# Two more weight places for the experts, laid at the end of the work area

## The chip, the cores and the metric

The kernel runs on one core of a Trainium2 chip. The metric is the device time of one execution in microseconds (us). The program is one launch, written engine by engine: TensorE (PE), VectorE (DVE), ScalarE (ACT), GpSimd (POOL) and the sync engine (SP) each have their own instruction stream, and they meet only at semaphores.

## The reference

Three transformer blocks follow one another on 256 tokens of width 1024, all in float32. The change concerns the mixture of experts of the first block: 32 experts, four of them for each token.

```python
def clamped_swiglu(gu):
    gate = jnp.minimum(gu[..., :D_FF], SWIGLU_LIMIT)
    lin = jnp.clip(gu[..., D_FF:], -SWIGLU_LIMIT, SWIGLU_LIMIT)
    return gate * jax.nn.sigmoid(SWIGLU_ALPHA * gate) * (lin + 1)

def moe_ffn(h, w_router, b_router, w_gu, b_gu, w_down, b_down):
    logits = (h @ w_router + b_router).astype(jnp.float32)
    top_val, top_idx = lax.top_k(logits, TOP_K)
    gate_w = jax.nn.softmax(top_val, axis=-1).astype(h.dtype)
...
    def expert_block(args):
        xb, e = args
        gu = xb @ w_gu[e] + b_gu[e]
        return clamped_swiglu(gu) @ w_down[e] + b_down[e]
```

Each expert has a w_gu of 1024 x 2048 and a w_down of 1024 x 1024, 12 MiB together.

## The kernel before

**Weights.** All weights of the three blocks lie in HBM as one stream of pieces, each 128 partitions x 2048 float32, 1 MiB. A ring in SBUF has four places (`SLOTS`). SP alone loads it: it waits until `pieces_used` says that the piece that lay in a place four pieces earlier has been multiplied, then issues one DMA for the next piece into that place. TensorE waits on the semaphore of the place (`ring_full_0` to `_3`) before it multiplies, and raises `pieces_used` behind the piece's last matmul. Piece n lies in place n % 4.

**Experts.** With these inputs no expert has more than 64 tokens, apart from the fullest one, which is run twice; so the `narrow` path runs: 33 items (`ITEMS`), one after another, in a hardware loop on each engine. An item is 12 pieces, j0 to j11: j0 to j7 are w_gu (L793), j8 to j11 are w_down (L822). What TensorE does in an item, in its order:

- j0 and j1 (L793); the scatter of the item before (`scatter`, L761); its exit matrix turned (`exits`, L767)
- j2 and j3; the gather of the next item's tokens (`gather`, L751); a turned block of the hidden rows (`turned`, L772)
- j4 and j5; a turned block; j6 and j7; two turned blocks
- j8 to j11 (L822); then the next item's j0

ACT copies the hidden rows out of PSUM (L2168), makes the sigmoids (L2173) and copies the result of an item (L2189), and DVE does the bias, the clamps and the products (L1548 to L1559). The last of the 33 items repeats the fullest expert: SP reads its number with one load of a value (L1279) and issues the 12 pieces from lines of its own (L1282).

**The work area.** `work` is one tensor of 128 partitions x 32768 float32 in which each stage lays its own tiles. From the places that `plan` takes for the first block, its mixing part reaches column 27528 and the `narrow` path column 20117.

Of the kernel before, what the change touches and what calls it, by code (L numbers as in the profile page):

```python
# [30 lines left out]
D = 1024  # L31
DC = D // P
HD = 64
SLOTS = 4
SLOT = 2048
SCALE = HD ** -0.5
MASKED = -1e30
# [115 lines left out]
def build(nc, stages, dram, known):  # L153
# [6 lines left out]
    with ctx:  # L160
# [86 lines left out]
            return got  # L247


        ring_full = [sem(f"ring_full_{s}") for s in range(SLOTS)]  # L250
        used = signal("pieces_used")
        ones_set, silu_of_c = signal("ones_set"), signal("silu_of_c")
        masks_set = signal("masks_set")
# [239 lines left out]
        def _(pe):  # L493
# [7 lines left out]
            def piece(name, i=0):  # L501

                n = place[name, i]
                pe.wait_ge(ring_full[n % SLOTS], 16 * (n // SLOTS + 1))
                return ring[:, n % SLOTS, :]

            def conditioning(s, a, b, fresh=False):

# [226 lines left out]
            def narrow(m):  # L735
# [45 lines left out]
                with pe.Fori(0, ITEMS) as e:  # L781
                    for i in range(4):
                        if i == 0:
                            pe.wait_ge(nar_xe, e + 1)
                        if i >= 2:
                            pe.wait_ge(nar_g, e * 4 + (i - 1))
                        for h in range(2):
                            n = base + 2 * i + h
                            pe.wait_ge(ring_full[n % SLOTS], e * 48 + 16 * (n // SLOTS + 1))
                            w = ring[:, n % SLOTS, :].rearrange("p (c g o) -> p c g o", c=4, g=2)  # L790
                            for c in range(4):
                                for g in range(2):
                                    mm = pe.matmul(psum[g * SEATS:(g + 1) * SEATS, 4 + i % 2, 0:256],  # L793
                                                   m["xe"][:, 4 * h + c, :], w[:, c, g, :],
                                                   start=(h == 0 and c == 0), stop=True, skip_group_check=True)
                            mm.then_inc(used.sem, 1)
                        if i == 0:
                            pe.wait_ge(nar_y, e + 1)
                            scatter()
                            pe.wait_ge(nar_ge, e + 1)  # L800
                            exits()
                        if i == 1:
                            pe.wait_ge(nar_lv, e + 1)
                            pe.wait_ge(nar_en, e + 2)
                            gather()
                        if i >= 1:
                            pe.wait_ge(nar_g, e * 4 + i)
                            if i >= 2:
                                pe.wait_ge(nar_b, e * 4 + (i - 1))
                            turned(i - 1)  # L810
                    pe.wait_ge(nar_g, e * 4 + 4)
                    pe.wait_ge(nar_b, e * 4 + 3)
                    turned(3)
                    pe.wait_ge(nar_xe, e + 2)
                    for k in range(4):
                        n = base + 8 + k
                        pe.wait_ge(ring_full[n % SLOTS], e * 48 + 16 * (n // SLOTS + 1))
                        pe.wait_ge(nar_act, e * 4 + (k + 1))
                        w = ring[:, n % SLOTS, :].rearrange("p (f o) -> p f o", f=2)
                        for f in range(2):  # L820
                            for h in range(2):
                                mm = pe.matmul(psum[h * SEATS:(h + 1) * SEATS, 7, :], m["act_e"][:, 2 * k + f, :],  # L822
                                               w[:, f, h * 512:(h + 1) * 512], start=(k == 0 and f == 0), stop=True,
                                               skip_group_check=True)
                        mm.then_inc(used.sem, 1)
# [3 lines left out]
            def wide(m):  # L829
# [13 lines left out]
                with pe.Fori(0, E_N) as e:  # L843
                    for j in range(8):
                        n = base + j
                        pe.wait_ge(ring_full[n % SLOTS], e * 48 + 16 * (n // SLOTS + 1))
                        h = j % 2
                        if h == 0:
                            pe.wait_ge(moe_free, e * 8 + (j + 2))
                        w = ring[:, n % SLOTS, :].rearrange("p (c g o) -> p c g o", c=4, g=2)  # L850
                        for k in range(2):
                            for g in range(2):
                                for c in range(4):
                                    mm = pe.matmul(psum[:, 4 + (j - h + k) % 4, g * T:(g + 1) * T],
                                                   w[:, c, g, k * P:(k + 1) * P], hT[:, 4 * h + c, :],
                                                   start=(h == 0 and g == 0 and c == 0), stop=True,
                                                   skip_group_check=True)
                        mm.then_inc(used.sem, 1)
                    for k in range(4):
                        n = base + 8 + k  # L860
                        pe.wait_ge(ring_full[n % SLOTS], e * 48 + 16 * (n // SLOTS + 1))
                        pe.wait_ge(moe_v, e * 40 + 5 * (2 * k + 2))
                        w = ring[:, n % SLOTS, :].rearrange("p (f o) -> p f o", f=2)
                        for f in range(2):
                            for c in range(DC):
                                mm = pe.matmul(acc[:, c, :], w[:, f, c * P:(c + 1) * P], m["act"][:, 2 * k + f, :],
                                               start=False, stop=False, skip_group_check=True)
                        mm.then_inc(used.sem, 1)
                for k in range(12):

                    n = base + 12 * E_N + k
                    pe.wait_ge(ring_full[n % SLOTS], 16 * (n // SLOTS + 1))
# [379 lines left out]
        def _(sp):  # L1252
            stream = dram["stream"]

            def send(n, k):

                sp.wait_ge(used.sem, n - SLOTS + 1)
                sp.dma_start(ring[:, n % SLOTS, :], stream[k]).then_inc(ring_full[n % SLOTS], 16)

            def sent(first, last, back):  # L1260

# [7 lines left out]
                for n in range(b * SLOTS, last):  # L1269
                    send(n, n - back)  # L1270

            for s in range(SLOTS):
                sp.dma_start(ring[:, s, :], stream[s]).then_inc(ring_full[s], 16)
            if 1 in stages:
                base = first_piece["moe"]
                again = base + 12 * E_N
                sent(SLOTS, again, 0)
                sp.wait_ge(*at("flag_set"))
                fullest = sp.value_load(A[1]["flag"][0:1, 1:2], min_val=0, max_val=E_N - 1)  # L1279
                for k in range(12):  # L1280
                    sp.wait_ge(used.sem, again + k - SLOTS + 1)
                    sp.dma_start(ring[:, (again + k) % SLOTS, :], stream[fullest * 12 + (base + k)]) \  # L1282
                      .then_inc(ring_full[(again + k) % SLOTS], 16)
                sent(again + 12, n_pieces, 12)
            else:
                sent(SLOTS, n_pieces, 0)

# [3 lines left out]
        def _(ve):  # L1291
# [521 lines left out]
            def peer():  # L1813
# [92 lines left out]

                def u_low(s):

                    slot = (first_piece["peer"] + s) % SLOTS
                    ve.tensor_tensor(ring_parts[:, slot, 0:D], ring[:, slot, 0:D], m["u_high"][:, s % 2, :].bitcast(F32), ALU.subtract) \  # L1910
                      .then_inc(blk_ul, 1)

                ve.wait_ge(*at("zeroed"))
# [11 lines left out]
                def block(s, n, last=False):  # L1925

                    if not last:
# [12 lines left out]
                    slot = (first_piece["peer"] + s) % SLOTS  # L1940
                    ve.wait_ge(blk_h, n + 1)
                    ve.tensor_tensor(ring_parts[:, slot, D:2 * D], ring[:, slot, D:2 * D], m["v_high"][:, s % 2, :].bitcast(F32), ALU.subtract) \  # L1942
                      .then_inc(blk_w, 1)

                with ve.Fori(0, PE_N // 4 - 1) as i:
# [101 lines left out]
        def _(sc):  # L2047
# [235 lines left out]
            def peer():  # L2283
# [51 lines left out]
                def landed(s):  # L2335
                    return ring_full[(base + s) % SLOTS], 16 * ((base + s) // SLOTS + 1)

                sc.wait_ge(*landed(0))
                u_high(0)
                for s in range(4):  # L2340

                    sc.wait_ge(*landed(s + 1))
                    if s >= 1:
                        sc.wait_ge(blk_a, s)
                    u_high(s + 1)
# [3 lines left out]
                    gelu(s)  # L2349
                with sc.Fori(1, PE_N // 4 - 1) as i:  # L2350
                    for s in range(4):
                        full, count = landed(s + 1)
# [6 lines left out]
                for s in range(4):  # L2359
                    n = PE_N - 4 + s  # L2360
                    if s < 3:
                        sc.wait_ge(*landed(n + 1))
# [339 lines left out]
```

## Time and profile before

| | us |
|---|---|
| median of 3 runs | 3379.26 |
| lowest and highest run | 3374.78, 3379.7 |
| profiled execution, its own time | 3371.07 |
| its span in the trace | 3369.3 |

The page of the profile gives, for 40 equal slices of the span (84.2 us each), how busy each engine was, the TensorE clock that was granted, and what the DMA engines moved. Counted from 0, slices 6 to 16 lie wholly in the experts' stage. A view of windows gives the same numbers for any stretch, the timeline gives the instructions in order, each with the idle time before it and what ended that, and the view of one tile tells how long a DMA took from its issue to its landing. Ends of matmuls are modelled, so starts are the firmer reading.

### The profile page before, as it was taken

To read this page: it belongs to the slowest core of one execution; us is meant where nothing else is said; L and a number is where in the kernel's file an instruction comes from. 1 tells how busy PE (TensorE), PEld (TensorE's weight loads), DVE (VectorE), ACT (ScalarE), POOL (GpSimd) and SP (SyncE) were. 2 spreads that over 40 slices of the span, in tenths; PEclk is the share of its full clock that TensorE was granted. 3 is DMA by queue.
4 is the path that set the end of the run, shared out by engine and by line. 5 is a ranking of instruction groups with operands and counts; after the bars stand their busy time and mean duration, and the time that the engine had idled before them with its cause. 6 is when DMAs were issued, how large, how long until landed. Compare 5 with 4: busy or idle time off the path is not lost.

```text
span 3369.3 us, 55104 instructions
## 1 busy us (share of the span) xinstructions
PE 3013.5 (89%) x21350; PEld 2375.7 (71%) x21350; DVE 1281.4 (38%) x2809; ACT 867.9 (26%) x1464; POOL 127.3 (4%) x85
## 2 busy tenths in 40 slices
PE   7999899999999999988999518899999999889998
PEld 5678655555455454547788417799999999767887
DVE  1520212122221222222411589866666666521330
ACT  2310112212222222221411004444444444321110
POOL 0000000000000000000000016500000000000000
PEclk9999889999999999999999759999999999879999
DMA  5664579999999999984654200045545555423342
GB/s 233 263 252 155 197 297 386 398 385 392 397 386 397 389 384 398 377 360 152 236 221 142 88 0 0 0 167 182 187 176 185 183 178 186 164 75 125 138 150 88
DMA packets 105299, 763.89 MB, mean 227 GB/s; under 512 B 11776, under 2 KB 11776, under 8 KB 12672
## 3 DMA queue, kind: packets, MB, share of 16 engines
q1 hardware_dynamic: 103536, 753.97, 58.3%
q0 software_dynamic: 1680, 8.72, 0.7%
q8 instruction: 63, 1.03, 0.1%
q14 instruction: 20, 0.16, 0.0%
HBM read 760.55 MB, written 2.10 MB: 226 GB/s over the span
## 4 chain that ended last, share of the span: by engine, by line
PE 79%; DMA 9%; DVE 8%; issue 2%; ACT 1%; DVEq 0%; POOL 0%; SPq 0%; ACTq 0%; POOLq 0%
PE psum L554 20%; PE psum L793 13%; PE psum L1163 11%; PE psum L1172 11%; DMA weight_ring<-in_stream 9%; PE psum L751 4%; PE psum L822 3%; DVE chunkbuf L1887 3%; PE psum L1229 2%; PE psum L570 2%; PE psum L761 2%; PE psum L516 2%; PE psum L545 1%; PE psum L772 1%; DVE work L1293 1%
## 5 line engine op out<-in xcount | busy, mean ns | idle before, releaser
L793 PE MATMUL psum<-weight_ring,work 128*64 128x256 f32 x4224 | 494.5, 384 | 37.0 <-DMA weight_ring<-in_stream 36.2
L554 PE MATMUL psum<-hT,weight_ring 128*128 128x256 f32 x2240 | 505.0, 388 | 15.5 <-ACT hT L2049 15.5
L554 PEld LDWEIGHTS psum<-hT,weight_ring 128*128 128x128 f32 x2240 | 436.0, 195 | 80.9 <-issue 18.7
L793 PEld LDWEIGHTS psum<-weight_ring,work 128*64 128x64 f32 x4224 | 290.0, 137 | 226.5 <-DMA weight_ring<-in_stream 78.9
L1548 DVE TENSOR_TENSOR work<-psum,work 128x256 f32<-128x256 f32 x132 | 56.2, 426 | 810.6 <-PE psum L772 810.6
L822 PE MATMUL psum<-weight_ring,work 128*64 128x512 f32 x1056 | 248.2, 602 | 28.7 <-DMA weight_ring<-in_stream 28.4
L1172 PE MATMUL psum<-peer_parts,v_high 128*128 128x256 f32 x2048 | 266.8, 283 | 0.3 <-DVE ring_parts L1942 0.2
L1172 PEld LDWEIGHTS psum<-peer_parts,v_high 128*128 128x128 f32 x2048 | 254.9, 192 | 0.7 <-DVE ring_parts L1942 0.7
L822 PEld LDWEIGHTS psum<-weight_ring,work 128*64 128x64 f32 x1056 | 66.6, 136 | 186.8 <-DMA weight_ring<-in_stream 96.8
L554 PE MATMUL psum<-work,weight_ring 128*128 128x256 f32 x800 | 175.9, 382 | 5.4 <-DVE work L1293 3.0
L1922 DVE TENSOR_TENSOR chunkbuf<-chunkbuf,work 128x256 f32<-128x256 f32 x128 | 81.7, 638 | 240.0 <-ACT chunkbuf L2324 240.0
L554 PEld LDWEIGHTS psum<-work,weight_ring 128*128 128x128 f32 x800 | 152.9, 192 | 27.6 <-DVE work L1293 3.8
L2049 ACT ACTIVATE work<-psum 128x512 f32<-128x512 f32 (+4 forms) x107 | 67.5, 638 | 381.8 <-PE psum L554 338.0
L1910 DVE TENSOR_TENSOR ring_parts<-weight_ring,peer_parts 128x1024 fp32r<-128x1024 f32 x128 | 156.8, 1225 | 15.3 <-ACT peer_parts L2332 10.7
L2332 ACT ACTIVATE peer_parts<-weight_ring 128x1024 fp32r<-128x1024 f32 x128 | 135.9, 1063 | 94.6 <-DMA weight_ring<-in_stream 94.6
L1942 DVE TENSOR_TENSOR ring_parts<-weight_ring,v_high 128x1024 fp32r<-128x1024 f32 x128 | 156.0, 1219 | 0.0
L1887 DVE TENSOR_TENSOR chunkbuf<-vec,chunkbuf 128x512 f32<-128x512 f32 x128 | 153.7, 1246 | 4.9 <-PE psum L1120 3.3
L1163 PE MATMUL psum<-h_high,peer_parts 128*128 128x256 f32 x1024 | 144.9, 284 | 4.9 <-DVE ring_parts L1910 4.9
L2168 ACT ACTIVATE work<-psum 128x256 f32<-128x256 f32 x132 | 51.1, 387 | 368.9 <-PE psum L793 368.9
L1163 PE MATMUL psum<-h_low,peer_parts 128*128 128x256 f32 x1024 | 144.5, 284 | 0.0
L1163 PE MATMUL psum<-h_high,ring_parts 128*128 128x256 f32 x1024 | 144.5, 284 | 0.0
L1172 PE MATMUL psum<-peer_parts,ring_parts 128*128 128x256 f32 x1024 | 143.7, 283 | 0.0
(251 smaller groups left out, 3626.1 us busy)
## 6 DMA issues: line engine op xcount, KB each, us to landing
weight_ring<-in_stream SPq DMA_DIRECT2D x719, 1024.0 KB, 6.5
work<-in_rows POOLq DMA_DIRECT2D x1, 1312.0 KB, 16.9
xT<-in_x POOLq DMA_DIRECT2D x1, 1024.0 KB, 9.8
work<-in_ctx POOLq DMA_DIRECT2D x1, 1024.0 KB, 18.9
x_spill<-xT POOLq DMA_DIRECT2D x1, 1024.0 KB, 7.4
xT<-x_spill POOLq DMA_DIRECT2D x4, 256.0 KB, 6.8
out_x<-xT POOLq DMA_DIRECT2D x4, 256.0 KB, 2.9
work<-in_moe POOLq DMA_DIRECT2D x1, 768.0 KB, 6.7
```

Source lines behind the costliest of these rows:

```text
L554: mm = pe.matmul(ps[:, j * T:(j + 1) * T], w[:, c, j * P:(j + 1) * P], moving[:, c, :], start=(j == 0 and c == 0), stop=True, skip_group_c ...
L751: mm = pe.matmul(psum[:, 7, c * SEATS:(c + 1) * SEATS], m["x_nat"][:, t, c * P:(c + 1) * P], m["en"][:, t, :], start=(c == 0 and t == 0), ...
L793: mm = pe.matmul(psum[g * SEATS:(g + 1) * SEATS, 4 + i % 2, 0:256], m["xe"][:, 4 * h + c, :], w[:, c, g, :], start=(h == 0 and c == 0), st ...
L822: mm = pe.matmul(psum[h * SEATS:(h + 1) * SEATS, 7, :], m["act_e"][:, 2 * k + f, :], w[:, f, h * 512:(h + 1) * 512], start=(k == 0 and f = ...
L1163: mm = pe.matmul(psum[:, 4 + s % 4, 0:T], u[:, c * P:(c + 1) * P], h[:, c, :], start=(k == 0 and c == 0), stop=True, skip_group_check=True)
L1172: mm = pe.matmul(acc[:, c, :], v[:, c * P:(c + 1) * P], m[wt][:, s % 2, :], start=False, stop=False, skip_group_check=True)
L1887: ve.tensor_tensor(place, m["v"]["iota"].unsqueeze(1).to_broadcast([P, CHUNK, PE_N]), m["idxT"][:, q, bass.ds(at0 + t * P, CHUNK)].unsquee ...
L1910: ve.tensor_tensor(ring_parts[:, slot, 0:D], ring[:, slot, 0:D], m["u_high"][:, s % 2, :].bitcast(F32), ALU.subtract) \
L1922: ve.tensor_tensor(m["wt"][:, s % 2, :], m["ge"][:, s % 2, :], G[:, :, bass.ds(n, 1)].rearrange("p t a -> p (t a)"), ALU.mult).then_inc(bl ...
L1942: ve.tensor_tensor(ring_parts[:, slot, D:2 * D], ring[:, slot, D:2 * D], m["v_high"][:, s % 2, :].bitcast(F32), ALU.subtract) \
L2049: sc.activation(out_, in_, func, **kw).then_inc(*A_.up(*names))
L2332: sc.activation(m["u_high"][:, s % 2, :], ring[:, (base + s) % SLOTS, 0:D], ACT.Copy) \
```

## The change

While the experts run, the ring has six places instead of four (`MORE = 2`). Places 4 and 5 are the last 4096 columns of `work`, from column 28672. Within an item, piece j lies in place j % 6 (for places below four, counted from where the ring stands), and 12 is a multiple of six, so that every item finds its pieces in the same places. SP issues a piece of the experts when the piece six before it has been multiplied. For the first item j0 to j3 go out under the old condition, j4 and j5 directly behind j3, and from j6 on the new condition holds. Behind the experts the ring has four places again. `landed` works out what the semaphore of a place counts to, and `landed_of` does it for item e of a loop.

```diff
 SLOTS = 4
+MORE = 2
 SLOT = 2048
...
-        ring_full = [sem(f"ring_full_{s}") for s in range(SLOTS)]
+        ring_full = [sem(f"ring_full_{s}") for s in range(SLOTS + MORE)]
+
+
+        moe_at = first_piece["moe"]
+        moe_end = moe_at + 12 * ITEMS
+        more = work[:, 32768 - MORE * SLOT:32768].rearrange("p (s k) -> p s k", s=MORE)
+        assert moe_at % SLOTS == moe_end % SLOTS and 12 % (SLOTS + MORE) == 0
+        loads = 12 // (SLOTS + MORE)
+
+        def place_of(n):
+            if moe_at <= n < moe_end:
+                s = (n - moe_at) % 12 % (SLOTS + MORE)
+                return s if s >= SLOTS else (moe_at + s) % SLOTS
+            return n % SLOTS
+
+        def slot(n):
+            s = place_of(n)
+            return ring[:, s, :] if s < SLOTS else more[:, s - SLOTS, :]
+
+        def landed(n):
+
+            s = place_of(n)
+            if n < moe_at:
+                return ring_full[s], 16 * (n // SLOTS + 1)
+            past = len([k for k in range(moe_at) if k % SLOTS == s]) if s < SLOTS else 0
+            if n < moe_end:
+                e, j = divmod(n - moe_at, 12)
+                return ring_full[s], 16 * (past + loads * e + j // (SLOTS + MORE) + 1)
+            return ring_full[s], 16 * (past + loads * ITEMS + (n - moe_end) // SLOTS + 1)
+
+        def landed_of(n, e):
+
+            full, count = landed(n)
+            return full, e * (16 * loads) + count
...
                n = place[name, i]
-                pe.wait_ge(ring_full[n % SLOTS], 16 * (n // SLOTS + 1))
-                return ring[:, n % SLOTS, :]
+                pe.wait_ge(*landed(n))
+                return slot(n)
...
                            n = base + 2 * i + h
-                            pe.wait_ge(ring_full[n % SLOTS], e * 48 + 16 * (n // SLOTS + 1))
-                            w = ring[:, n % SLOTS, :].rearrange("p (c g o) -> p c g o", c=4, g=2)
+                            pe.wait_ge(*landed_of(n, e))
+                            w = slot(n).rearrange("p (c g o) -> p c g o", c=4, g=2)
...
                        n = base + 8 + k
-                        pe.wait_ge(ring_full[n % SLOTS], e * 48 + 16 * (n // SLOTS + 1))
+                        pe.wait_ge(*landed_of(n, e))
                         pe.wait_ge(nar_act, e * 4 + (k + 1))
-                        w = ring[:, n % SLOTS, :].rearrange("p (f o) -> p f o", f=2)
+                        w = slot(n).rearrange("p (f o) -> p f o", f=2)
...
                 sp.wait_ge(used.sem, n - SLOTS + 1)
-                sp.dma_start(ring[:, n % SLOTS, :], stream[k]).then_inc(ring_full[n % SLOTS], 16)
+                sp.dma_start(slot(n), stream[k]).then_inc(landed(n)[0], 16)
...
+            def item(at_once, piece_of, e=0):
+
+                for j in range(12):
+                    n = moe_at + j
+                    if at_once and j >= SLOTS + MORE:
+                        sp.wait_ge(used.sem, n - (SLOTS + MORE) + 1)
+                    elif at_once and j < SLOTS:
+                        sp.wait_ge(used.sem, n - SLOTS + 1)
+                    elif not at_once:
+                        sp.wait_ge(used.sem, e * 12 + (n - (SLOTS + MORE) + 1))
+                    sp.dma_start(slot(n), piece_of(j)).then_inc(landed(n)[0], 16)
+
             for s in range(SLOTS):
                 sp.dma_start(ring[:, s, :], stream[s]).then_inc(ring_full[s], 16)
             if 1 in stages:
-                base = first_piece["moe"]
-                again = base + 12 * E_N
-                sent(SLOTS, again, 0)
+                sent(SLOTS, moe_at, 0)
+                item(True, lambda j: stream[moe_at + j])
+                with sp.Fori(1, E_N) as e:
+                    item(False, lambda j: stream[e * 12 + (moe_at + j)], e)
                 sp.wait_ge(*at("flag_set"))
                 fullest = sp.value_load(A[1]["flag"][0:1, 1:2], min_val=0, max_val=E_N - 1)
-                for k in range(12):
-                    sp.wait_ge(used.sem, again + k - SLOTS + 1)
-                    sp.dma_start(ring[:, (again + k) % SLOTS, :], stream[fullest * 12 + (base + k)]) \
-                      .then_inc(ring_full[(again + k) % SLOTS], 16)
-                sent(again + 12, n_pieces, 12)
+                item(False, lambda j: stream[fullest * 12 + (moe_at + j)], E_N)
+                sent(moe_end, n_pieces, 12)
```

The same two replacements are made in `wide`, which does not run here, and two names that the new functions would hide are changed on DVE and ACT.

The instructions of SP, from the end of the pieces ahead of the experts, before. The loop of L1268 sends every piece up to the last but one item, four at a time; L1282 sends the repeated expert.

```order
L1268 ISA [waits pieces_used]
L1268 DMA weight_ring<-in_stream 128x2048
L1265 REGISTER_ALU
L1265 COMPARE_AND_BRANCH
L1279 TENSOR_LOAD work [waits vector_done_ffn1]
L1279 ISA x2
L1282 ISA [waits pieces_used]
L1282 DMA weight_ring<-in_stream 128x2048
```

The same place in the changed kernel: the first item's twelve pieces, and the start of the loop over the other items (L1316; the branch is L1323's).

```order
L1316 DMA weight_ring<-in_stream 128x2048 [waits pieces_used] x4
L1316 DMA work<-in_stream 128x2048 x2
L1316 DMA weight_ring<-in_stream 128x2048 [waits pieces_used] x4
L1316 DMA work<-in_stream 128x2048 [waits pieces_used] x2
L1323 UNCONDITIONAL_BRANCH
L1323 ISA
L1316 ISA [waits pieces_used]
L1316 DMA weight_ring<-in_stream 128x2048
```

SP's code is longer, and the two DMAs into `work` of the first item wait for nothing of their own. The number and the order of the pieces are the same.

TensorE at the end of an item (j8 to j11), before:

```order
L822 MATMUL psum<-weight_ring,work 64x512 [waits narrow_activations,ring_full_0]
L822 MATMUL psum<-weight_ring,work 64x512 x3
L822 MATMUL psum<-weight_ring,work 64x512 [waits narrow_activations,ring_full_1]
L822 MATMUL psum<-weight_ring,work 64x512 x3
L822 MATMUL psum<-weight_ring,work 64x512 [waits narrow_activations,ring_full_2]
L822 MATMUL psum<-weight_ring,work 64x512 x3
L822 MATMUL psum<-weight_ring,work 64x512 [waits narrow_activations,ring_full_3]
L822 MATMUL psum<-weight_ring,work 64x512 x3
```

and in the changed kernel:

```order
L856 MATMUL psum<-weight_ring,work 64x512 [waits narrow_activations,ring_full_2,narrow_tokens_copied]
L856 MATMUL psum<-weight_ring,work 64x512 x3
L856 MATMUL psum<-weight_ring,work 64x512 [waits narrow_activations,ring_full_3]
L856 MATMUL psum<-weight_ring,work 64x512 x3
L851 REGISTER_ALU
L856 MATMUL psum<-work 64x512 [waits narrow_activations,ring_full_4]
L856 MATMUL psum<-work 64x512 x3
L856 MATMUL psum<-work 64x512 [waits narrow_activations,ring_full_5]
L856 MATMUL psum<-work 64x512 x3
```

The matmuls stand as before. The last two pieces are read from `work`, and their semaphores are those of the new places.

## Rows read from the trace of the kernel before

**Rows 1.** The page, busy tenths in 40 slices, and rates

```profile
PE   7999899999999999988999518899999999889998
...
PEclk9999889999999999999999759999999999879999
DMA  5664579999999999984654200045545555423342
GB/s 233 263 252 155 197 297 386 398 385 392 397 386 397 389 384 398 377 360 152 236 221 142 88 0 0 0 167 182 187 176 185 183 178 186 164 75 125 138 150 88
```

**Rows 2.** Windows: the experts, two stretches of one item, a later stage

```profile
core 0: us, PE busy (x) PEld busy (x) DVE busy (x) ACT busy (x) POOL busy (x), PEclk, DMA share, GB/s
434.50:1500.20 1065.70, 977.07 (x7194) 555.60 (x7194) 230.98 (x792) 225.16 (x428) 0.00 (x0) 1.00 0.96 387
717.00:742.00 25.00, 22.83 (x162) 12.75 (x164) 3.39 (x13) 5.24 (x9) 0.00 (x0) 1.00 1.01 424
742.00:748.00 6.00, 6.00 (x56) 3.70 (x52) 3.03 (x11) 0.73 (x3) 0.00 (x0) 1.00 0.79 264
...
2200.00:2900.00 700.00, 700.00 (x5835) 700.00 (x5835) 452.09 (x610) 291.76 (x365) 0.00 (x0) 1.00 0.51 182
```

**Rows 3.** Waits from 434.5 to 1500.3: total us, times, longest

```profile
PEld psum L822 <- DMA weight_ring<-in_stream: 96.8, 89, 1.7
...
PEld psum L793 <- DMA weight_ring<-in_stream: 78.9, 64, 2.1
...
PE psum L793 <- DMA weight_ring<-in_stream: 36.2, 64, 1.2
...
PE psum L822 <- DMA weight_ring<-in_stream: 28.4, 58, 0.8
```

**Rows 4.** Timeline of PE, 700 to 770: start, length, instructions, idle before

```profile
700.32 0.44 PE L767 MATMUL psum<-ident,work 128*128 128x128 f32 x2
...
708.23 3.67 PE L793 MATMUL psum<-weight_ring,work 128*64 128x256 f32 x32
711.83 0.44 PE L772 MATMUL psum<-ident,work 128*128 128x128 f32 x2
...
717.30 3.67 PE L822 MATMUL psum<-weight_ring,work 128*64 128x512 f32 x16
721.52 1.94 PE L822 MATMUL psum<-weight_ring,work 128*64 128x512 f32 x8 [0.55 <-DMA weight_ring<-in_stream]
724.00 1.94 PE L822 MATMUL psum<-weight_ring,work 128*64 128x512 f32 x8 [0.55 <-DMA weight_ring<-in_stream]
726.47 1.95 PE L793 MATMUL psum<-weight_ring,work 128*64 128x256 f32 x16 [0.53 <-DMA weight_ring<-in_stream]
728.96 1.95 PE L793 MATMUL psum<-weight_ring,work 128*64 128x256 f32 x16 [0.55 <-DMA weight_ring<-in_stream]
730.84 2.00 PE L761 MATMUL psum<-work 64*128 64x256 f32 x16
732.77 0.44 PE L767 MATMUL psum<-ident,work 128*128 128x128 f32 x2
...
749.75 3.65 PE L822 MATMUL psum<-weight_ring,work 128*64 128x512 f32 x16
...
762.90 2.00 PE L761 MATMUL psum<-work 64*128 64x256 f32 x16
764.83 0.43 PE L767 MATMUL psum<-ident,work 128*128 128x128 f32 x2
```

**Rows 5.** Issue to landing, four loads issued 723 to 732

```profile
DMA to landing us min/median/max: 7.8/7.8/7.8
```

**Rows 6.** The same, one load issued at 742.8

```profile
DMA to landing us min/median/max: 5.2/5.2/5.2
```

**Rows 7.** The same, six loads issued 403 to 416

```profile
DMA to landing us min/median/max: 7.5/9.5/10.0
```

**Rows 8.** Timeline of ACT and DVE around j8 to j0

```profile
719.37 0.29 DVE L1559 TENSOR_TENSOR work<-work 128x128 f32<-128x128 f32 x1
...
725.99 0.60 ACT L2189 ACTIVATE work<-psum 128x512 f32<-128x512 f32 x1 [6.90 <-PE psum L822]
726.61 1.28 ACT L2168 ACT_TABLE_LOAD   x1
```

**Rows 9.** Timeline of PE: first j0, last pieces, what follows

```profile
434.50 6.11 PE L793 MATMUL psum<-weight_ring,work 128*64 128x256 f32 x32 [0.77 <-ACT work L2157]
...
1498.29 1.94 PE L822 MATMUL psum<-weight_ring,work 128*64 128x512 f32 x8 [0.56 <-DMA weight_ring<-in_stream]
1500.92 2.00 PE L761 MATMUL psum<-work 64*128 64x256 f32 x16 [0.70 <-ACT work L2189]
1507.88 5.36 PE L545 MATMUL psum<-work,ones 128*128 128x256 f32 x16 [4.96 <-ACT work L2049]
```

More of the change, by code:

```diff
@@ L845, in wide @@
                         n = base + j
-                        pe.wait_ge(ring_full[n % SLOTS], e * 48 + 16 * (n // SLOTS + 1))
+                        pe.wait_ge(*landed_of(n, e))
                         h = j % 2
@@ L849, in wide @@
                             pe.wait_ge(moe_free, e * 8 + (j + 2))
-                        w = ring[:, n % SLOTS, :].rearrange("p (c g o) -> p c g o", c=4, g=2)
+                        w = slot(n).rearrange("p (c g o) -> p c g o", c=4, g=2)
                         for k in range(2):
@@ L860, in wide @@
                         n = base + 8 + k
-                        pe.wait_ge(ring_full[n % SLOTS], e * 48 + 16 * (n // SLOTS + 1))
+                        pe.wait_ge(*landed_of(n, e))
                         pe.wait_ge(moe_v, e * 40 + 5 * (2 * k + 2))
-                        w = ring[:, n % SLOTS, :].rearrange("p (f o) -> p f o", f=2)
+                        w = slot(n).rearrange("p (f o) -> p f o", f=2)
                         for f in range(2):
@@ L871, in wide @@
                     n = base + 12 * E_N + k
-                    pe.wait_ge(ring_full[n % SLOTS], 16 * (n // SLOTS + 1))
+                    pe.wait_ge(*landed(n))
                     pe.matmul(psum[0:1, 4, 0:2], ones[:, 0:1], ones[:, 0:2], start=True, stop=True,
@@ L1907, in u_low @@
                 def u_low(s):
-                    slot = (first_piece["peer"] + s) % SLOTS
-                    ve.tensor_tensor(ring_parts[:, slot, 0:D], ring[:, slot, 0:D], m["u_high"][:, s % 2, :].bitcast(F32), ALU.subtract) \
+                    at0 = (first_piece["peer"] + s) % SLOTS
+                    ve.tensor_tensor(ring_parts[:, at0, 0:D], ring[:, at0, 0:D], m["u_high"][:, s % 2, :].bitcast(F32), ALU.subtract) \
                       .then_inc(blk_ul, 1)
@@ L1938, in block @@
                     ve.tensor_tensor(low, wt, high.bitcast(F32), ALU.subtract).then_inc(blk_w, 1)
-                    slot = (first_piece["peer"] + s) % SLOTS
+                    at0 = (first_piece["peer"] + s) % SLOTS
                     ve.wait_ge(blk_h, n + 1)
-                    ve.tensor_tensor(ring_parts[:, slot, D:2 * D], ring[:, slot, D:2 * D], m["v_high"][:, s % 2, :].bitcast(F32), ALU.subtract) \
+                    ve.tensor_tensor(ring_parts[:, at0, D:2 * D], ring[:, at0, D:2 * D], m["v_high"][:, s % 2, :].bitcast(F32), ALU.subtract) \
                       .then_inc(blk_w, 1)
@@ L2333, in u_high, with in_ring @@
                       .then_inc(blk_uh, 1)
-                def landed(s):
-                    return ring_full[(base + s) % SLOTS], 16 * ((base + s) // SLOTS + 1)
-                sc.wait_ge(*landed(0))
+                def in_ring(s):
+                    return landed(base + s)
+                sc.wait_ge(*in_ring(0))
                 u_high(0)
                 for s in range(4):
-                    sc.wait_ge(*landed(s + 1))
+                    sc.wait_ge(*in_ring(s + 1))
                     if s >= 1:
@@ L2351, in peer @@
                     for s in range(4):
-                        full, count = landed(s + 1)
+                        full, count = in_ring(s + 1)
                         sc.wait_ge(full, i * 16 + count)
@@ L2361, in peer @@
                     if s < 3:
-                        sc.wait_ge(*landed(n + 1))
+                        sc.wait_ge(*in_ring(n + 1))
                         sc.wait_ge(blk_a, n)
```

## The prediction, as it was made before the changed kernel ran

> **What bounds the kernel now.** I read the page first. TensorE is busy nearly everywhere, and in the experts' slices, 6 to 16 counted from 0, the DMA engines are too (a 9 in each, 377 to 398 GB/s); in no other stage do both stand high [rows 1]. So the experts have two candidates for a bound, and an average over slices can't choose between them. The windows give the stage's measure: from the first j0 at 434.50 to the end of the last j11 at 1498.29 + 1.94 = 1500.23 [rows 9] it takes 1065.7 us, 32.29 us for each of 33 items, at 387 GB/s, and with TensorE busy for 977 us [rows 2].
>
> Then I looked inside one item. From 717 to 742 the DMA engines move 424 GB/s, from 742 to 748 only 264 [rows 2]. The reader is to see that the link isn't at its limit all the time: once in each item it runs short of requests. The waits of the stage say that TensorE in turn waits for loads: 36.2 + 28.4 us before matmuls, in 64 + 58 waits, all of them on the ring [rows 3]. The timeline shows where. After j3 and the long gather the ring is full and TensorE sets the pace; at 721.52, 724.00, 726.47 and 728.96 each piece (j10, j11, j0, j1) starts only when its load has landed [rows 4]. So in one half of an item the link starves for places, in the other TensorE starves for pieces. That is what a ring too short for uneven use looks like. The two costs are one: what the link loses at 742 is missing when j9 to j1 want it.
>
> **How fast could each of the two go alone.**
>
> TensorE: two pieces without a wait take 711.83 - 708.23 = 3.60 us. The six pieces j8 to j1 take 730.84 - 717.30 = 13.54 us where 3 x 3.60 = 10.80 would do. The whole item, from L767 to L767, took 764.83 - 732.77 = 32.06 us, and the one ahead of it 732.77 - 700.32 = 32.45. In the item of 32.06 the six pieces took 762.90 - 749.75 = 13.15 [rows 4]. Without the waits: 32.06 - 2.35 = 29.71, and 32.45 - 2.74 = 29.71 us.
>
> Link: three landings in a row are 728.96 - 721.52 = 7.44 us apart [rows 4], 2.48 us for each 1 MiB piece, or 29.76 us for twelve. By the window, 12 x 1.0486 MB / 424 GB/s = 29.68 us [rows 2].
>
> So both limits are about 29.7 us, 2.5 us under today's item.
>
> **What six places do.** From 730.84 to 749.75 TensorE works 18.91 us on six pieces and other matmuls [rows 4], and the link could bring 18.91 / 2.48 = 7.6 pieces. In the next six pieces, 10.80 us, it brings 4.35. About 1.65 pieces must be stored over the item. With four places, one is being multiplied and one lies empty for the time that a load needs from issue to landing beyond its own 2.48 us: 5.2 us in all for a load that finds nothing ahead of it [rows 6]. Two are left for the 1.65, and those two also hold the loads in flight. The link's loss of 32.29 - 29.76 = 2.53 us per item is one piece. Two more places are more than that piece, and more than the 1.65. A load then waits longer behind others, which costs nothing: with three in flight it lands after 7.8 us [rows 5], and where SP sent more, ahead of the experts, after up to 10.0 [rows 7], which is 2.2 us, less than one landing interval, more.
>
> **The sum.** As both limits nearly coincide, a landing that comes late isn't caught up by a faster partner, so I take 29.9 us per item, 0.14 over the larger of the two. The first item starts at half the clock: its first two pieces take 6.11 us and not 3.67 [rows 9, 4], 2.4 us that stay. New stage: 33 x 29.9 + 2.4 = 989.1 us. Gain: 1065.7 - 989.1 = 76.6 us.
>
> *Bounds of the unknown terms.* At best 29.71 us per item: 982.8, a gain of 82.9. At worst for a part that the trace doesn't show: TensorE never went from j11 to j0 without a wait for a load, so the loop's end may hold a cost of its own; it is at most 726.47 - 724.00 - 1.80 = 0.67 us, which would make 30.4 us and a gain of 60.1. I take nearly nothing for it, because the later stage with loops of matmuls shows 700.00 us busy in 700 [rows 2].
>
> *Costed at nothing.* (1) What other engines do for TensorE in the shortened half. The last activation for j11 is ready at 719.37 + 0.29 = 719.66; j11 would start at 717.30 + 5.40 = 722.70. The result of an item is copied (0.60 us) and a table loaded (1.28) within 1.90 us of the last piece's end [rows 8]; the scatter that reads the copy stands two pieces later, 3.60 us, and the first hidden rows are copied then, too. Cover left: 1.7 us. (2) SP's longer code, its extra register instructions and the load of the fullest expert's number: up to five requests are now ahead of TensorE, over 9 us. (3) j4 and j5 of the first item, sent early: 5 us of link time between 415 and 434.5, in which TensorE doesn't wait for the link. (4) What follows: the first piece behind the experts is sent on the same condition as before, and TensorE goes from 1500.92 through waits for ACT [rows 9] that no load takes part in; the rest moves forward as a block.
>
> The profiled execution took 3371.07 us, the median of the runs is 8.2 us over it, and I keep that distance: 3371.07 - 76.6 + 8.2 = 3302.7, forecast **3302 us**.
>
> **One rule weighed.** The windows hold 424 GB/s over 25 us and 387 over the stage [rows 2]; this is what the second limit rests on. The Trainium skill (HBM Reference, Specifications (TRN2)) gives about 425 GB/s for a core that streams alone, set by its 16 DMA engines; by that estimate twelve pieces take 29.6 us and the gain would be 1065.7 - 33 x 29.71 - 2.4 = 82.9, TensorE being the slower then.
>
> **The rivals.**
>
> *The link has less to give than a 25 us window promises.* The DMA engines' busy share is 0.96 over the stage [rows 2]; if busy means full, only 0.04 x 1065.7 = 43 us are left: 3336 us. If the 264 GB/s at 742 is the memory's own hiccup after a burst, nothing is left: 3379. Against both: the dip comes once per item, behind the gather, when SP has nothing to send, and the share reads 1.01 where 424 GB/s move and still 0.79 where 264 do, so it counts packets that are slow to start. The Trainium skill (DMA: Bandwidth & Descriptors, Where 436 GB/s comes from) says that loads from HBM are held to about 358 GB/s by the memory; by that rule the stage would be past its limit already and nothing would change. The stage's 387 GB/s says otherwise. Chances: 0.10 for the first, 0.07 for no change.
>
> *Another engine's chain takes the wait's place.* If the 1.7 us of cover is not there, or the loop's end costs more than 0.67 us, an item takes 30.4 to 31 us: 3319 to 3339 us. 0.08.
>
> *Slower: TensorE's clock.* It works with fewer pauses, and the granted clock could fall in this stage. Below 29.71 / 32.29 = 0.92 the item is longer than now; at 0.90 it is 33.0 us, the stage 1091.8, the time 3405 us. Against it: 700 us with TensorE busy throughout at a granted 1.00 [rows 2]. The lower digits stand at the stages' seams, where it pauses [rows 1]. 0.03.
>
> **How the numbers follow.** The forecast's own range, 29.7 to 30.4 us per item, is 3296 to 3319 us and has 0.70; 0.02 is for a larger gain. The range for 8 in 10 takes in most of the other engine's chain and a few us of spread between runs: 3290 to 3334. Two runs of this kernel differ by 5 us, so 0.2%, 7 us, is about what can be told from no change. Faster by more: 0.70 + 0.02 + 0.10 + 0.08 = 0.90; within: 0.07; slower: 0.03.
>
> **What would show it.** In the changed kernel's profile an item, L795 to L795, takes 29.7 to 30.2 us, and the stage ends near 1424. Over the stage the link moves 415 GB/s or more, with no stretch of 6 us below 380. The waits of TensorE for loads fall from 122 to a few tens, short ones, or it waits as often but briefly, if the link is the slower by a hair. Loads land 10 to 15 us after their issue, still 2.48 us apart. Wrong, if landings move apart, if the clock of the stage is below 1.00, or if a new wait (ACT's copy before L795, the table load) stands at the item's seam. All stages from 1500 on keep their lengths.

## The result, and the profile after

| | before | changed |
|---|---|---|
| median, us | 3377.02 (4 runs, 3374.0 to 3379.7) | 3284.74 (4 runs, 3282.43 to 3287.05) |
| profiled execution, its own time | 3371.07 | 3284.36 |
| its span | 3369.3 | 3282.6 |
| the experts, first j0 to end of last j11 | 1065.7 | 984.3 |
| the span without them | 2303.6 | 2298.3 |

The ratio is 0.9727 with a 95% interval of 0.971 to 0.9744. Forecast were 3302 us and a range of 3290 to 3334. The direction and the mechanism hold; the time lies 5.3 us under the range.

The page of the changed kernel, busy tenths and rates in 40 slices, answers to [rows 1]:

```profile
PE   7999899999999999989999058899999999789998
...
DMA  5664489999999999956634000155445555423442
GB/s 240 260 266 148 169 330 422 422 422 422 422 422 422 422 422 422 422 198 264 241 142 150 17 0 0 52 180 186 183 179 181 186 182 179 143 82 124 146 149 90
```

Eleven slices in a row, 6 to 16, read exactly 422 GB/s, where they read 377 to 398 before, and windows of 6 us, from 464 to 506 and from 1380 to 1410, read 418 to 429, so the dip once in each item is gone. (The link is the path from HBM through the DMA engines to SBUF.) The windows of the stage, and of two stretches of 25 us, answer to [rows 2]; the clock stays at 1.00, 2.4 GHz:

```profile
core 0: us, PE busy (x) PEld busy (x) DVE busy (x) ACT busy (x) POOL busy (x), PEclk, DMA share, GB/s
433.00:1417.30 984.30, 954.82 (x7194) 564.86 (x7194) 230.94 (x792) 224.77 (x428) 0.00 (x0) 1.00 1.00 417
700.00:725.00 25.00, 24.04 (x198) 15.43 (x196) 5.35 (x19) 6.52 (x12) 0.00 (x0) 1.00 1.01 422
725.00:750.00 25.00, 24.78 (x190) 14.80 (x188) 4.35 (x15) 5.33 (x9) 0.00 (x0) 1.00 1.01 422
```

The timeline of TensorE in an item of the first six, and in a later one (start, length, instructions, idle time before); it answers to [rows 4]:

```profile
529.20 0.44 PE L801 MATMUL psum<-ident,work 128*128 128x128 f32 x2
...
546.18 3.65 PE L856 MATMUL psum<-weight_ring,work 128*64 128x512 f32 x16
549.67 3.60 PE L856 MATMUL psum<-work 128*64 128x512 f32 x16
553.10 3.62 PE L827 MATMUL psum<-weight_ring,work 128*64 128x256 f32 x32
556.65 2.00 PE L795 MATMUL psum<-work 64*128 64x256 f32 x16
558.58 0.44 PE L801 MATMUL psum<-ident,work 128*128 128x128 f32 x2
```

```profile
737.27 0.44 PE L801 MATMUL psum<-ident,work 128*128 128x128 f32 x2
...
761.17 1.90 PE L827 MATMUL psum<-weight_ring,work 128*64 128x256 f32 x16
763.29 1.95 PE L827 MATMUL psum<-weight_ring,work 128*64 128x256 f32 x16 [0.22 <-DMA weight_ring<-in_stream]
765.17 2.00 PE L795 MATMUL psum<-work 64*128 64x256 f32 x16
767.10 0.44 PE L801 MATMUL psum<-ident,work 128*128 128x128 f32 x2
```

The early item takes 558.58 - 529.20 = 29.38 us without a wait. There the six pieces j8 to j1, 546.18 to 556.65, take 10.47 us (13.15 and 13.54 before). The later one takes 767.10 - 737.27 = 29.83, with a short wait at j0 and at j1. Twelve landings at 2.485 us are 29.82. So the stage has two parts: up to the sixth item TensorE sets the pace, from the seventh on the link. The waits of TensorE for loads from 610 to 1417.3 answer to [rows 3] (total us, times, longest); of the 64.6 us before matmuls (PE), 5.8 are left, and of the 175.7 before weight loads (PEld), 27.1:

```profile
PEld psum L827 <- DMA weight_ring<-in_stream: 27.1, 54, 0.7
PE psum L827 <- DMA weight_ring<-in_stream: 5.8, 27, 0.2
```

A load into the four places of the ring now takes this long from issue to landing, 610 to 1400, where a queued one took 7.8 us before [rows 5]; one into the two new places takes 8.4 to 11.7:

```profile
DMA to landing us min/median/max: 9.3/11.0/12.8
```

### The profile page after: what moved, and what is told of

The parts are those of the page before. It is cut to its first block, busy times and chain, and to the rows that moved or that the text cites. A ratio compares the mean times of both kernels' runs of the same rounds, so it can differ in the third digit from the quotient of the medians.

```text
span 3282.6 us, 54818 instructions
## 1 busy us (share of the span) xinstructions
PE 2987.1 (91%) x21350; PEld 2382.4 (73%) x21350; DVE 1281.0 (39%) x2809; ACT 866.6 (26%) x1464; POOL 127.3 (4%) x85
## 4 chain that ended last, share of the span: by engine, by line
PE 78%; DMA 10%; DVE 8%; issue 2%; ACT 1%; DVEq 0%; POOL 0%; SPq 0%; ACTq 0%; POOLq 0%
PE psum L588 21%; PE psum L827 13%; PE psum L1197 11%; PE psum L1206 11%; DMA weight_ring<-in_stream 9%; PE psum L785 4%; DVE chunkbuf L1931 3%; PE psum L1263 2%; PE psum L604 2%; PE psum L795 2%; PE psum L550 2%; PE psum L579 2%; PE psum L856 1%; DVE work L1337 1%; ACT work L2093 1%
## 5 line engine op out<-in xcount | busy, mean ns | idle before, releaser
L827 PE MATMUL psum<-weight_ring,work 128*64 128x256 f32 x3168 | 370.7, 384 | 6.6 <-DMA weight_ring<-in_stream 5.8
L827 PEld LDWEIGHTS psum<-weight_ring,work 128*64 128x64 f32 x3168 | 220.3, 137 | 146.0 <-DMA weight_ring<-in_stream 27.8
L2368 ACT ACTIVATE chunkbuf<-psum 128x256 f32<-128x256 f32 x128 | 49.2, 384 | 348.0 <-PE psum L1197 348.0
L1197 PEld LDWEIGHTS psum<-h_high,peer_parts 128*128 128x128 f32 x1024 | 133.1, 193 | 5.7 <-issue 5.7
```

What stands on the lines that cost most here:

```text
L1197: mm = pe.matmul(psum[:, 4 + s % 4, 0:T], u[:, c * P:(c + 1) * P], h[:, c, :], start=(k == 0 and c == 0), stop=True, skip_group_check=True)
```

## The experiments

Each starts from the changed kernel unless it says otherwise. The length of the stage is read from the profiled execution of each, as in the table above. The experiments ran on three chips, each beside the kernel before on the same chip, so ratios and stages compare across the table better than medians do.

| run | median, us | ratio to before, 95% interval | stage, us | span without it |
|---|---|---|---|---|
| six places, wait of four | 3372.44 | 1.0003 (0.9989 to 1.0016) | 1067.7 | 2311.8 |
| six places, wait of five | 3287.87 | 0.9768 (0.9749 to 0.9787) | 988.0 | 2295.2 |
| no head start | 3288.52 | 0.9762 (0.9747 to 0.9777) | 985.2 | 2305.7 |
| twelve places | 3274.96 | 0.9719 (0.9703 to 0.9736) | 972.0 | 2300.3 |
| half loads, four places | 3288.39 | 0.9751 (0.9726 to 0.9776) | 984.9 | 2303.4 |
| light gather, four places | 3286.41 | 0.9752 (0.9726 to 0.9778) | 986.3 | 2296.4 |
| light gather, six places | 3279.72 | 0.9722 (0.9699 to 0.9745) | 981.3 | 2300.5 |
| the changed kernel again | 3286.05 | 0.9736 (0.9713 to 0.9758) | 984.4 | 2299.5 |
| twelve places again | 3277.66 | 0.9712 (0.9688 to 0.9737) | 972.4 | 2303.9 |
| twelve places, wait of eight | 3283.97 | 0.9733 (0.9709 to 0.9756) | 980.0 | 2299.6 |

The kernel before had medians of 3371.11 (beside the waits of four and five, no head start and the first twelve places), 3372.61 (half loads and light gather) and 3374.7 us (the last three).

### The depth alone: the wait of four, and of five

```diff
                     n = moe_at + j
-                    if at_once and j >= SLOTS + MORE:
-                        sp.wait_ge(used.sem, n - (SLOTS + MORE) + 1)
-                    elif at_once and j < SLOTS:
-                        sp.wait_ge(used.sem, n - SLOTS + 1)
-                    elif not at_once:
-                        sp.wait_ge(used.sem, e * 12 + (n - (SLOTS + MORE) + 1))
+                    if at_once:
+                        sp.wait_ge(used.sem, n - (SLOTS if j < SLOTS else 4) + 1)
+                    else:
+                        sp.wait_ge(used.sem, e * 12 + (n - 4 + 1))
```

The second has 5 in place of the last two 4. With the wait of four j4 and j5 of the first item are no longer sent ahead, with the wait of five only j4 is.

> The changed kernel with its six places and all its new code, but SP waits as for a ring of four (a piece of the experts is sent when the piece four before it has been multiplied). Theory (the gain is the depth of the ring): the item goes back to 32.2 to 32.5 us, the time to 3370 to 3382 us. Rival (the gain lies in where the loads go, in the new loops of SP or in code placement): it stays below 3350.

> The same with the wait of a ring of five. Theory: five places already cover what one item must store, so that the link still paces nearly all items at 29.8 us; against the changed kernel only the stock ahead is one piece (2.5 us) smaller: 3286 to 3293 us. Rival (every place is worth the same, half of the gain each): 3330 us.

With the wait of four, and the rest of the change in place but for that head start, the time is that of the kernel before, ratio 1.0003. Where the loads go, SP's longer code and the other registers cost and bring nothing that this interval (0.9989 to 1.0016) would show. The fifth place alone brings the stage from 1067.7 to 988.0 us, the sixth another 3.7, of which the head start is a part (see below). The places are not worth the same: what counts is whether the ring holds what has to be stored over one item.

### What the head start is worth

```diff
-                    elif at_once and j < SLOTS:
+                    elif at_once:
```

> The changed kernel, but j4 and j5 of the first item wait for j0 and j1, as before, and are not sent ahead. Theory (from the seventh item on the stage is paced by the link, 2.485 us for each piece, so that what the link has not brought before the stage begins it must bring inside it): 2 x 2.485 = 5 us more, 3287 to 3292 us. Rival (TensorE paces the stage): no difference, within 2 us of the changed kernel.

The time is in the range that was expected, but the stage says otherwise: 985.2 against 984.3 us, 0.9 and not 5. (Its first two pieces took 0.95 us less, at half the clock for a shorter time; with that added, it is 1.8.) The windows from 434 to 480, of the changed kernel and of this one, show why:

```profile
434.00:480.00 46.00, 45.28 (x348) 28.66 (x346) 8.29 (x29) 9.77 (x19) 0.00 (x0) 0.96 0.86 337
```

```profile
434.00:480.00 46.00, 45.20 (x354) 28.66 (x352) 8.91 (x31) 9.80 (x19) 0.00 (x0) 0.98 0.93 379
```

With a full ring SP has nothing to send. The link of the changed kernel idles at the start, and the other makes up 46 x (379 - 337) / 1000 = 1.9 MB, 1.8 of its two missing pieces. What is sent ahead into a ring that would fill anyway is not won in full. It does change the first items: without the head start they take 29.69, 29.80 and 29.86 us (L801 to L801), the link's pace nearly from the start, where the changed kernel has 29.38 or 29.39 four times.

### More places

```diff
-MORE = 2
+MORE = 8
...
-        more = work[:, 32768 - MORE * SLOT:32768].rearrange("p (s k) -> p s k", s=MORE)
+        more = work[:, 32768 - 6 * SLOT:32768].rearrange("p (s k) -> p s k", s=6)
+        spare = chunkbuf[:, 0:8, :].rearrange("p a b -> p (a b)").rearrange("p (s k) -> p s k", s=2)
...
-            return ring[:, s, :] if s < SLOTS else more[:, s - SLOTS, :]
+            return ring[:, s, :] if s < SLOTS else more[:, s - 4, :] if s < 10 else spare[:, s - 10, :]
```

The wait of eight adds the edit of the waits above, with 8.

> Twelve places: four of the ring, six at the end of the work area, two in the tile chunkbuf, which no stage before the second block's uses; SP waits for the piece twelve before. (The path for crowded experts, which does not run with these inputs, would need part of these columns.) Theory: the larger stock lasts for all 33 items, every item takes TensorE's own 29.4 us, the stage 972 to 975 us against 984: 3272 to 3277 us, with few waits for loads after the first item. Rival (six places take all there is): within 3 us of the changed kernel. Second rival (more loads in flight slow the link or TensorE): above 3290.

> The twelve places again, on the same chip as the changed kernel. Theory: the stage takes 972 us again with 29.39 us for each item, 12.3 us under the changed kernel (ratio 0.9722). Rival (the difference between chips made it): within 4 us of the changed kernel.

> The same twelve places, but SP waits for the piece eight before. Theory (stock): each item at TensorE's own 29.39 us takes 0.43 us of link time out of the stock; six places lasted to the sixth item, two more places hold 4.97 us, eleven to twelve items more: 29.39 us up to about item 17 or 18 and 29.82 behind it, the stage 979 us, 5 us under the changed kernel. Rival (six places are as good as any number that does not reach the end): 984. Second rival (eight are as good as twelve): 972.

> The changed kernel as it is, beside the kernel before on the same chip, five rounds. The traces so far give the stage of the experts 81.4 us less and the rest of the program differences of either sign. Theory (all of the change is in the stage): ratio 0.9759, about 3290 us where the kernel before takes 3371. Rival (something outside the stage gains 5 to 10 us more): 0.973, 3280.

Twelve places give 972.0 and 972.4 us, 12 under the changed kernel. In the second of these runs the list of waits from 440 to 1402 holds none of TensorE for a load. An item there (L802 to L802):

```profile
702.71 0.44 PE L802 MATMUL psum<-ident,work 128*128 128x128 f32 x2
...
732.10 0.44 PE L802 MATMUL psum<-ident,work 128*128 128x128 f32 x2
```

That is 29.39 us. In time, twelve places measure 8.4 us under the changed kernel on the same chip (3277.66 against 3286.05); the two ratios have overlapping intervals, and the stage decides. This is the fastest version here. The path for crowded experts reaches column 24597 and would need 4117 of the columns that it uses.

With the wait of eight, the stage is 980.0 us where 979 was expected, and the pace changes in the middle. Its L802 of successive items:

```profile
823.53 0.44 PE L802 MATMUL psum<-ident,work 128*128 128x128 f32 x2
...
852.91 0.44 PE L802 MATMUL psum<-ident,work 128*128 128x128 f32 x2
...
882.51 0.44 PE L802 MATMUL psum<-ident,work 128*128 128x128 f32 x2
...
912.32 0.44 PE L802 MATMUL psum<-ident,work 128*128 128x128 f32 x2
```

29.38, 29.60, 29.81: the stock, the pieces in the ring that are ahead of TensorE, ends in the sixteenth item (17 or 18 were expected). From 440 to 870 TensorE waits for no load, from 910 to 1413 it does so 16 times before matmuls. The link is the slower of the two by 0.43 us per item; a place beyond what an item needs should buy 2.485 / 0.43 = 5.8 items at TensorE's pace, so two should buy eleven or twelve, and they bought ten: from the sixth item to the sixteenth.

### Each partner relieved

Half loads, from a kernel with four places and the old conditions (`MORE = 0`):

```diff
-                    sp.dma_start(slot(n), piece_of(j)).then_inc(landed(n)[0], 16)
+                    sp.dma_start(slot(n)[:, 0:1024], piece_of(j)[:, 0:1024]).then_inc(landed(n)[0], 16)
```

The light gather, once with those four places, once with six:

```diff
-                    for c in range(DC):
+                    for c in range(1):
                         for t in range(TT):
                             mm = pe.matmul(psum[:, 7, c * SEATS:(c + 1) * SEATS], m["x_nat"][:, t, c * P:(c + 1) * P],
```

> Four places and waits as in the kernel before, but each piece of the experts loads only the first half of its columns (512 KB), so that the expert products are made with weights that are half stale: the link has twice the time, TensorE's work is the same. Theory (TensorE alone needs 29.4 us for an item): 29.4 us from the second item on, the stage 972 to 976 us, the time 3280 +- 8 us, as with twelve places. Rival (TensorE itself needs the 29.7 us that were read from pairs with no wait, or more): 29.7 to 30.4 us, 10 to 33 us more than that.

> Four places and the waits of the kernel before; the gather makes 2 of its 16 matmuls, so that the experts get only an eighth of their inputs and the burst of TensorE without use of a piece is 3.2 us shorter (105 us less work over the stage). Theory (the link runs dry because TensorE holds the places during the gather): the dip is nearly gone, the item is set by the link at 29.8 to 30.6 us, the time 3300 to 3330 us. Rival (TensorE's total work sets it): 105 us less, 3272.

> The changed kernel with the gather cut to 2 of its 16 matmuls in the same way (105 us less work for TensorE). Theory (the link paces the stage at 2.485 us for each piece): 29.8 us for each item, the stage 977 to 984 us, the time 3277 to 3285, nearly nothing gained. Rival (TensorE paces it, the link has more to give): the item falls to 26.2 to 28 us, the time to 3180 to 3240.

**Half loads** miss their expectation: 984.9 us, not 972 to 976, and 29.8 us for an item on average, which is what the rival gave. The windows from 480 to 1400, and the waits and the landings in them:

```profile
480.00:1400.00 920.00, 891.08 (x6726) 526.05 (x6723) 214.84 (x738) 211.53 (x402) 0.00 (x0) 1.00 0.63 212
```

```profile
PEld psum L826 <- DMA weight_ring<-in_stream: 29.7, 50, 1.2
PE psum L826 <- DMA weight_ring<-in_stream: 6.1, 14, 0.8
```

```profile
DMA to landing us min/median/max: 3.4/4.7/6.0
```

The link moves 212 GB/s, half of what it can, and TensorE still waits before w_gu pieces. A load of half the size takes 4.7 us to land in the median and up to 6.0. With four places and a piece used every 1.72 us a place must be full again after 3 x 1.72 = 5.2 us, less the signals. So a short ring seems to cost not only by volume: the time that one load takes to land is a second price, and four places only just pay it. That is worked out from these rows; no run varies this time alone. Four of the items take 29.39 us, which bounds TensorE's own need from above and speaks against the rival; the twelve places settle it.

**Light gather.** The gather takes 0.66 us and not 3.79, so that 33 x 3.13 = 103 us of TensorE's work are gone from the stage. (The gather for the first item lies ahead of the stage; it takes 1.08 us and not 7.06, so some 6 us of the times in the table are won outside.) With six places the stage falls by only 3.1 us against the changed kernel again, to 981.3: the link is the bound, as expected. With four places the item is 29.8 to 29.9 us from the third on, inside what I expected of it, but the time is 3286 us and not 3300 to 3330: the dip isn't nearly gone but gone. The rival, 3272 from TensorE's total work, fails as well: from 480 to 1400 TensorE waits 46.2 + 29.2 us for loads before matmuls. Windows from 480 to 1400, four places and six:

```profile
480.00:1400.00 920.00, 822.08 (x5860) 419.36 (x5862) 214.73 (x738) 210.71 (x401) 0.00 (x0) 1.00 1.01 422
```

```profile
480.00:1400.00 920.00, 822.08 (x5876) 420.02 (x5872) 213.75 (x734) 210.53 (x400) 0.00 (x0) 1.00 1.01 422
```

Both read 822.08 us busy and 422 GB/s. Four places suffice to fill the link when the gather between j3 and j4 is short. This fits the account that the old ring lost its time to the length of the gather, but it doesn't prove that alone: the light gather also takes 3.13 us of work from each item and so makes TensorE the faster partner by far, and no run here shortens the burst without shortening the item. The half loads show that the time of a load to land has a share, too.

## Why the prediction was right and where it was wrong

**What bounds the kernel** was read rightly: two limits close together and a ring too short to couple them. The wait of four shows that it is the depth, the light gather with six places shows the limit of the link, and the twelve places show TensorE's. That it is the gather that makes the use uneven is read from the timeline; the light gather with four places fits it. That about one stored piece was lacking agrees as well: the fifth place gave 79.7 of the 83.4 us between a wait of four and of six.

**The sum.** Forecast were 29.9 us per item, 989.1 for the stage and a gain of 76.6; measured are 984.3 and 81.4. Two terms were off. (1) TensorE's own item was taken as 29.71 us, from pairs of w_gu pieces at 3.60. Run without a wait, two w_down pieces take 727.92 - 724.43 = 3.49 us and the next two 3.43:

```profile
724.43 3.65 PE L856 MATMUL psum<-weight_ring,work 128*64 128x512 f32 x16
727.92 3.60 PE L856 MATMUL psum<-work 128*64 128x512 f32 x16
731.35 1.90 PE L827 MATMUL psum<-weight_ring,work 128*64 128x256 f32 x16
```

The item is 29.39 us. The gain of 82.9 us that I called the best held for six places (81.4) only because the link was slower; twelve places gain 93.7. As the link limits 27 of the 33 items, this brought only 6 x 0.43 = 2.6 us. (2) The 0.14 us that I added because a late landing would not be caught up were not needed: the paced items take 29.82 us, just twelve landings, 0.08 under the 29.9, or 2.6 us over the stage. The larger of two limits holds by itself once there is stock.

**The step that failed** is the last one, "the median of the runs is 8.2 us over it, and I keep that distance". The changed kernel's profiled execution stands 0.4 us under the median of its four runs; in the other runs that distance lay between 8.8 us over (wait of four) and 2.9 under (wait of five). A profiled execution is one draw. With 0.4 us in place of 8.2, the range would have begun at 3282 and held the measured time. Of the 17.3 us between 3302 and 3284.74, the distance makes 8.2 - 0.4 = 7.8, the rest of the span, 5.3 us shorter in the profiled execution, makes 5.3, and the item's term 4.8 (0.7 of the sum of these was rounded away in the forecast). Taken from the median of before's four runs, 3377.02, the forecast would have been 3300.4, and the measured time would still lie 15.7 us lower: the spread of the runs and of the rest of the program belonged in the range, whose lower end stood 6 us under the supposed best case.

**Where the rest of the span varies.** The span without the stage ran from 2295.2 to 2311.8 us over these kernels, whose code there is the same but for the first gather of the light ones. One stretch shows a piece of it: the second block, from one matmul to the same later one, in twelve places again and in the changed kernel.

```profile
1541.90:1633.09 91.19, 87.81 (x804) 67.70 (x800) 40.53 (x122) 31.34 (x79) 0.00 (x0) 0.96 0.62 235
1614.00:1618.00 4.00, 4.00 (x11) 3.06 (x10) 3.65 (x14) 0.00 (x0) 0.00 (x0) 0.50 0.69 285
```

```profile
1552.98:1640.87 87.89, 84.51 (x805) 65.26 (x801) 40.53 (x122) 31.35 (x79) 0.00 (x0) 1.00 0.66 250
```

The granted clock falls to 0.50, 1.2 GHz, for a few microseconds in the one, with TensorE busy throughout them, and stays at 1.00 in the other: 3.3 us. The medians gained 83 to 97 us over stages 78 to 94 us shorter. In each of the ten comparisons the median gained more than the stage, by 2.1 us (no head start) to 10.9 (the changed kernel at first); for the two light gathers some 6 us of that are the first gather. As all ten are taken against one trace of the kernel before, and the wait of four, whose median is the same within its interval, has a stage 2.0 us longer, a part may lie in that one reading. Whether a small real gain elsewhere stands behind the rest stays open.

**Costed at nothing.** The chains of ACT and DVE held. ACT's copy and table load in the changed kernel:

```profile
731.57 0.60 ACT L2233 ACTIVATE work<-psum 128x512 f32<-128x512 f32 x1 [5.36 <-PE psum L856]
732.18 1.28 ACT L2212 ACT_TABLE_LOAD   x1
```

They end at 733.46, and the scatter, TensorE's next use of the copy, starts at 735.34: 1.9 us of cover, 1.7 forecast. No new wait stands at the item's seam, and the loop's end costs TensorE nothing (j11 to j0 in 1.72 us).

**What was to show it.** The stage ended at 1417.3 (near 1424 was forecast), the link moved 417 GB/s over it (415 or more), TensorE waited 27 times before matmuls (122 before), and landings took 8.4 to 12.8 us (10 to 15), 2.485 apart. What follows the experts took 1865.3 us where it took 1869.1 before, and 1865.0 to 1875.9 in the other runs, so it kept its length within that spread. Two signs failed. The first five items were shorter than the 29.7 us given, four of them at 29.38 or 29.39. And "no stretch of 6 us below 380" did not hold in the first item, where the ring was full and SP had nothing to send:

```profile
434.00:440.00 6.00, 6.00 (x38) 3.56 (x36) 0.00 (x0) 0.57 (x2) 0.00 (x0) 0.66 0.34 113
440.00:446.00 6.00, 6.00 (x55) 4.04 (x51) 0.00 (x0) 1.24 (x3) 0.00 (x0) 1.00 0.80 304
```

**The rivals.** The link had more to give: 417 GB/s over the whole stage and 422 from 480 to 1400, and the stage gained 81.4 us, so neither 43 us nor nothing. The rule of about 425 GB/s for a core alone (the Trainium skill, HBM Reference, Specifications (TRN2)) agrees with it. The one of about 358 for loads from HBM (the Trainium skill, DMA: Bandwidth & Descriptors, Where 436 GB/s comes from) does not hold here: 422 were measured. The clock stayed at 1.00 with TensorE busy for 954.82 of 984.30 us, but for the first microseconds (0.66 from 434 to 440).

## What to carry to other kernels

Where two partners with nearly the same pace are coupled by a ring, compare the longest time that one of them works without freeing a place with what the ring stores. The course of one period, not the average, tells how many places are missing, and beyond that number a place buys only a fixed stock (here 2.485 us of link time). Look for the dip in the transfer rate inside one period; a busy share of 0.96 hid a twelfth of the link. And take medians for medians: the distance of one profiled execution from them is no property of the kernel.

## What was not expected of the hardware

- With the link as the limit an item takes 29.82 us, 2.485 for each load of 1 MiB, and the windows from 480 to 1400 read 421 to 422 GB/s with six places, with twelve, and with four where the gather is light. With twelve places a load takes up to 25.8 us to land, which is some ten in flight, and the rate is the same. The DMA engines' busy share reads 1.01 there and 0.97 at the 390 GB/s of the kernel before, so it is a poor measure of what is left.
- The shortest time from issue to landing was 4.7 us at 1 MiB (the kernel before, 480 to 1400); at half the size it was 3.4, with 4.7 in the median. Half the bytes did not halve it.
